# A two-layer encoder trunk on one core: the order of the four matmuls of each k tile, by column block instead of by half of the weights

## The reference

```python
D_MODEL = 2048; SEQ = 256; DEPTH = 2; D_FF = 4 * D_MODEL
...
def reference(x, ...):
    h = x
    for layer in range(DEPTH):
        hn = rms_norm(h, mix_norm[layer])
        if layer % N_MIXERS == 0:
            mix = swa_sink_attention(hn, ...)   # h @ w_qkv, ..., out @ w_o
        else:
            mix = rglru_block(hn, ...)          # h @ w_in, ..., @ w_out
        h = h + mix
        h = h + sqrelu_mlp(rms_norm(h, mlp_norm[layer]), mlp_w_up[layer], mlp_w_down[layer])
    return rms_norm(h, final_norm)
```

## Time and profile before

| | |
|---|---|
| time, median of 3 runs | 2031.53 us (2030.66 to 2032.17) |
| the profiled execution: time, and its span | 2030.48 us, 2028.6 us |
| PE busy / PEld busy | 1998.9 us (99%) / 1747.0 us (86%) |
| DVE busy / ACT busy | 1360.2 us (67%) / 1057.5 us (52%) |
| mean granted TensorE clock | 0.996 |
| read from HBM | 365.48 MB, 181 GB/s over the span |

### The profile page before, as it was taken

How to read it: one execution, slowest core, us unless ns; L and a number is a source line. 1 busy time by engine, 2 the same in 40 slices (tenths; PEclk the granted TensorE clock), 3 DMA queues, 4 the chain that set the end, 5 groups by cost and what they waited for, 6 DMA issues and landing times.

```text
span 2028.6 us, 34220 instructions
## 1 busy us (share of the span) xinstructions
PE 1998.9 (99%) x11604; PEld 1747.0 (86%) x11604; DVE 1360.2 (67%) x1560; ACT 1057.5 (52%) x1437; POOL 8.7 (0%) x12
## 2 busy tenths in 40 slices
PE   9999999999999999999999999999999999999997
PEld 8888888888888888888888888888888888888886
DVE  7777676656655665666688887666566556656665
ACT  7555554444444444445588886544444444444453
POOL 1000000000000000000000000000000000000000
PEclk9999999999999999999999999999999999999998
DMA  8433556656565655655655655565556556555652
GB/s 276 140 103 116 194 170 204 195 181 194 177 199 178 202 186 186 187 185 181 202 177 177 185 176 169 184 201 190 188 181 192 190 182 196 186 188 178 200 173 89
DMA packets 365879, 368.12 MB, mean 181 GB/s; under 512 B 11536, under 2 KB 363920, under 8 KB 365712
## 3 DMA queue, kind: packets, MB, share of 16 engines
q1 hardware_dynamic: 365552, 365.53, 56.9%
q0 software_dynamic: 288, 2.10, 0.3%
HBM read 365.48 MB, written 2.10 MB: 181 GB/s over the span
## 4 chain that ended last, share of the span: by engine, by line
PE 86%; DVE 6%; ACT 4%; issue 3%; ACTq 0%; DMA 0%; DVEq 0%; SPq 0%
PE ps L1256 55%; PE ps L1259 27%; DVE w_lo L766 2%; ACT w_hi L343 1%; PE aux L1276 1%; PE aux L1277 1%; PE aux L1278 1%; DVE u L780 1%; DVE u L1136 1%; DVE v L1100 1%; ACT L614 1%; ACT L634 0%; PE aux L1292 0%; PE aux L1329 0%; DVE driven L1098 0%
## 5 line engine op out<-in xcount | busy, mean ns | idle before, releaser
L766 DVE TENSOR_TENSOR w_lo<-w_raw,w_hi 128x1024 fp32r<-128x1024 f32 x678 | 817.1, 1222 | 341.4 <-ACT w_hi L343 340.4
L343 ACT ACTIVATE w_hi<-w_raw 128x1024 fp32r<-128x1024 f32 x678 | 702.1, 1054 | 435.1 <-PE ps L1259 432.3
L1256 PE MATMUL ps<-xn,w_hi 128*128 128x512 f32 x2880 | 908.5, 397 | 7.3 <-DVE w_lo L766 5.3
L1256 PE MATMUL ps<-mid,w_hi 128*128 128x512 f32 x2544 | 801.1, 396 | 5.3 <-DVE mid L1124 3.0
L1259 PEld LDWEIGHTS ps<-xn,w_lo 128*128 128x128 f32 x2880 | 541.7, 188 | 128.2
L1259 PEld LDWEIGHTS ps<-mid,w_lo 128*128 128x128 f32 x2544 | 478.5, 188 | 113.3
L1259 PE MATMUL ps<-xn,w_lo 128*128 128x256 f32 x2880 | 566.7, 278 | 0.0
L1259 PE MATMUL ps<-mid,w_lo 128*128 128x256 f32 x2544 | 500.3, 278 | 0.0
L1256 PEld LDWEIGHTS ps<-xn,w_hi 128*128 128x128 f32 x2880 | 439.6, 189 | 9.6 <-issue 8.8
L1256 PEld LDWEIGHTS ps<-mid,w_hi 128*128 128x128 f32 x2544 | 388.0, 189 | 6.5 <-issue 5.3
L780 DVE TENSOR_TENSOR u<-ps,half 128x512 f32<-128x512 f32 x170 | 117.4, 690 | 184.5 <-ACT half L356 162.5
(11 more groups left out here) (152 smaller groups left out, 804.6 us busy)
## 6 DMA issues: line engine op xcount, KB each, us to landing
w_raw<-mlp_w_up_dram SPq DMA_DIRECT2D x256, 512.0 KB, 3.8
w_raw<-mlp_w_down_dram SPq DMA_DIRECT2D x256, 512.0 KB, 3.4
w_raw<-b_w_in_dram SPq DMA_DIRECT2D x64, 512.0 KB, 3.9
w_raw<-a_w_qkv_dram SPq DMA_DIRECT2D x40, 512.0 KB, 5.4
w_raw<-a_w_o_dram SPq DMA_DIRECT2D x32, 512.0 KB, 3.8
w_raw<-b_w_out_dram SPq DMA_DIRECT2D x32, 512.0 KB, 4.4
h<-x_l_dram SPq DMA_DIRECT2D x4, 512.0 KB, 8.5
gate_raw<-b_gate_a_w_dram SPq DMA_DIRECT2D x8, 256.0 KB, 3.9
```

What stands on the lines that cost most here:

```text
L343: nc.scalar.activation(w_hi[:, s, :, :], w_raw[:, slot, :, :], ACT.Copy).then_inc(hi_ready, 1)
L766: nc.vector.tensor_tensor(w_lo[:, s, :, :], w_raw[:, slot, :, :], w_hi[:, s, :, :].bitcast(F32), ALU.subtract).then_inc(lo_ready, 1)
L1256: nc.tensor.matmul(ps[:, 2 * half_i + b, :], hi[:, k, b * PART:(b + 1) * PART], operand[:, :, kt, :], start=kt == 0, stop=False)
```

## The change

In each k tile, the four matmuls were ordered high b=0, high b=1, low b=0, low b=1. They are now high b=0, low b=0, high b=1, low b=1. The matmuls, their operands and their number stay the same.

```diff
                 for k in range(CH_KT):
                     kt = s * CH_KT + k
                     for b in range(2):
-                        nc.tensor.matmul(ps[:, 2 * half_i + b, :], hi[:, k, b * PART:(b + 1) * PART],
-                                         operand[:, :, kt, :], start=kt == 0, stop=False)
-                    for b in range(2):
-                        last = nc.tensor.matmul(ps[:, 2 * half_i + b, TOK:2 * TOK], lo[:, k, b * PART:(b + 1) * PART],
+                        cols = slice(b * PART, b * PART + PART)
+                        nc.tensor.matmul(ps[:, 2 * half_i + b, :], hi[:, k, cols], operand[:, :, kt, :],
+                                         start=kt == 0, stop=False)
+                        last = nc.tensor.matmul(ps[:, 2 * half_i + b, TOK:2 * TOK], lo[:, k, cols],
                                                 operand[:, 0, kt, :], start=False, stop=kt == KT - 1)
                 last.then_inc(wts_used, 1)
```

## The result

| | before | changed |
|---|---|---|
| median, 20 executions each | 2031.59 us | 2038.81 us |
| lowest to highest | 2028.26 to 2035.38 | 2027.63 to 2052.63 |
| ratio, 95% interval | | 1.0032 (1.0019 to 1.0046) |
| the profiled execution: time, span | 2030.48, 2028.6 us | 2038.83, 2036.9 us |

I had forecast no change (2031.5 us, within 0.2%), with 2015 to 2054 as the range. The median lies inside the range, but the kernel is slower by more than 0.2%, which I had given 0.30. The median hides the main thing: the 20 times of the changed kernel fall in clusters. Five lie from 2027.6 to 2029.0 us, three at 2036, nine from 2038.7 to 2042.0, three from 2051.8 to 2052.6. Before has nothing over 2035.4.

A forecast was written before the change was run, and what follows sets the result against it. PE's own matmuls were taken to bound the kernel (busy 1998.9 of 2028.6 us). All terms summed to 0 us, giving 2031.5 us against the median of before, with a range of 2015 to 2054 us.

The forecast's parts named there:

- Number of matmuls, DMA, waits, release of buffers: Whole kernel: no matmuls or loads added or removed, waits and release keep their places, DMA untouched; 0 us.
- Same bank twice in a row: Each low matmul adds to cells the matmul just before it wrote; taken as 0 us, upper bound 22 us.
- The evidence from the gates: Gate matmuls, three in a row into the same columns: the step changing bank is 0.12 us, mean 0.119; no penalty seen.
- the slower rival: Low behind its high in one bank, or each length change, costs a few ns: 2053 or 2039 us; chance 0.27.
- If the cost of a step is the longer of the load and the matmul with its fixed excess: In each group, two weight loads lie behind long matmuls and two behind short ones in both orders; 0 us.
- the excess: Time of a group of four matmuls beyond the array's own 0.64 us: 57 ns, 155 us of the kernel.
- What neighbours what: Long-long and short-short adjacencies become long-short ones: 16 us gain to 22 us cost for the shorts, taken as 0.
- The likeliest case: Whole kernel: order does not matter, 2031.5 us, within 4 us; chance 0.46.
- the weak place: The excess of 14 ns a matmul might hang on what follows what; the rows show one order only.

The follow-up runs named there:

- one_in_four: Changed kernel, but the first k tile of each chunk (one in four) in the order of before: 2036.68 us, ratio 1.0027 to before.
- one_in_sixteen: Changed kernel, but the first k tile of each pair (one in 16) in the order of before: 2038.46 us, ratio 1.0035 to before.
- old_new: Order of before in the first pair of each quad (32 k tiles), the new order in the second: 2029.29 us, ratio 0.9990 to before.
- runs_of_eight: Against the kernel before, each chunk does all eight high matmuls, then its eight low ones: 2036.21 us, ratio 1.0018.
- mlp0_only: Kernel before, with the new order in the first MLP alone: median 2041.54 us, ratio 1.0033 to before.
- reset_even: Changed kernel, but the first chunk of each quad (32 k tiles) as eight high, then eight low matmuls: 2050.36 us, ratio 1.0093 to before.
- reset_odd: As reset_even, but the next k tile after the eight lows is in the order of before: 2023.52 us, ratio 0.9957 to before.
- again: The changed kernel once more, no edit: median 2039.09 us, ratio 1.0039 to before; the profiled execution took 2025.47 us.

## Why the prediction was wrong, by its steps

- *Number of matmuls, DMA, waits, release of buffers: 0 us.* Right: PE's waits and ACT's wait for PE stayed within 6 us of before.
- *Same bank twice in a row: 0 us, at most 22.* Right, and shown: three of four steps in a bank cost nothing (ratio 0.9993). The evidence from the gates, no dip at the change of bank, was the right row. Both halves of the slower rival, as I had it, were the wrong mechanism with the right sign.
- *"If the cost of a step is the longer of the load and the matmul with its fixed excess, a group is 2 x 0.235 + 2 x 0.115 both times. 0 us."* This step failed. The counts of loads behind long and short matmuls are kept, as I wrote, but the excess, 57 ns of a group before, is not fixed: it is 53 ns in the short rhythm (0.693) and 66 in the long one (0.706).
- *"What neighbours what": 0 us between -16 and +22.* The bounds held and the choice between them did not. I had bracketed two effects of opposite sign and taken them to cancel at the mean; both exist, in different executions. That the bounds held is in part luck, since I had priced them on the shorts alone. By the starts in ns, over the stretches of 600 us, before has 0.2331 for a long and 0.1152 for a short, the short rhythm 0.2300 and 0.1167, the long one 0.2364 and 0.1170: the gain came in the longs, against dearer shorts, and about two thirds of the loss lie in the longs. (The 0.235 that I used is one group's; its neighbours have 0.232.) If both MLPs have the short rhythm the time is 2025 to 2029 us, if both have the long one 2051 to 2053, and 12 of the 20 executions lie between, as with one of each.
- *The likeliest case.* At even odds for each of two large stretches, two of these three outcomes would differ from before by more than 4 us on the slower side. The cost of the long rhythm, 10 ns a group, is also three times the gain of the short, 3.4. That is why the median is slower.

What I wrote at the end, that the rows show that order in one form only and that this is the weak place, was the weak place. There were two signs in the trace of before that I did not use: a run of shorts cost 0.119 and the pair 0.115, so a step's cost did hang on its neighbours, by more than the 0.8 ns a step from which I said a rival decides; and neighbouring groups, alike in their instructions, took 0.6958 and 0.6975 in turn. With that, 0.46 for "within 0.2%" was too much.

## What to carry to other kernels

Where one engine's stream is the bound, a new order of the same instructions can change its rate by a per cent with no wait in sight. Count instructions over long stretches without waits and compare the stretches with each other, not only the kernels: two rates for the same code within one trace say at once that there is a state. And where times come in clusters, a median of three tells little; break the long stretches with a pattern that ends in a known state, and this spread goes or can be turned to use. Then try the rule that comes out of one kernel on the traces of the others, as with the swap here.

## What the runs showed of the hardware that I had not expected

- fp32r matmuls of 512 and 256 columns in turn, each with its own 128x128 weights, run in one of two rhythms at the upper clock: 0.693 or 0.706 us for two of each. The rhythm lasted 600 us and more without a change, and a stream of 512, 512, 256, 256 has one rate, 0.697. One such group swapped the two rhythms each time when 6 or 30 pairs of 512 and 256 lay between (`one_in_four`, `one_in_sixteen`); sixteen of them behind 32 such pairs turned the long rhythm into the short and kept the short (`old_new`).
- A run of eight shorts goes to 0.119 each and leaves the stream in a known state. A group's worth of runs of eight costs 0.695 in the kernels that reset once a quad, and 0.698 where every chunk is of that kind (`runs_of_eight`).
- What the state is physically stays open, and so does what picks it where a stream begins. The same program took either rhythm behind the statistics matmuls of the first MLP, the long one in 9 of 12 executions of `mlp0_only`.
- The spread of the kernel before itself, 2028 to 2035 us, goes with the granted clock of the execution. Beside `reset_even` and `reset_odd` it took 2027.8 and 2028.2 us at 0.997, 2030.5 to 2031.7 at 0.996, 2033.1 and 2033.4 at 0.994, and 2035.0 to 2035.4 at 0.993; within a cluster the changed kernel does the same (2035.9 to 2036.0 at 0.997, 2038.7 and up at 0.996). Ahead of the last 20 us, the clock was at the lower level for 6.8 us in the profiled execution of before (0.996; from 10.6 to 14.0 us and from 208.6 to 212.0), for 3.4 us in that of `again` (0.997) and for 17.1 us in that of `mlp0_only` (0.993).
